# Latent attention in a two-layer block: 128 weight columns a head, keys and values apart, and the rotation read from the product's bank

## The reference

```python
cq = _rmsnorm(b_cq, gq)                       # 384 wide
ckv = _rmsnorm(b_ckv, gkv)                    # 256 wide
qh = _split_heads(cq @ w_uq, MLA_HEADS)       # 8 heads of 64 + 32 columns
q_b = jnp.concatenate([qh[..., :MLA_NOPE], _rope(qh[..., MLA_NOPE:], pos)], axis=-1)
kvh = _split_heads(ckv @ w_ukv, MLA_HEADS)    # 8 heads of 64 key + 64 value columns
k_rope = _rope(b_kr[:, None], pos)            # 32 columns, shared by the heads
k_b = jnp.concatenate([kvh[..., :MLA_NOPE],
                       jnp.broadcast_to(k_rope, (B, MLA_HEADS, S, MLA_ROPE))], axis=-1)
yb = mla_attention(q_b, k_b, kvh[..., MLA_NOPE:])
```

## Time and profile before

| | us |
|---|---|
| time, median of 3 runs | 1920.81 |
| the runs | 1924.45, 1920.81, 1919.28 |
| span of the profiled execution | 1919.6 |
| TensorE busy | 1839.1 |
| VectorE busy | 1327.5 |
| ScalarE busy | 959.1 |
| GpSimd busy | 61.7 |

### The profile page before, as it was taken

How to read it: one execution, slowest core, us unless ns; L and a number is a source line. 1 busy time by engine, 2 the same in 40 slices (tenths; PEclk the granted TensorE clock), 3 DMA queues, 4 the chain that set the end, 5 groups by cost and what they waited for, 6 DMA issues and landing times.

```text
span 1919.6 us, 34151 instructions
## 1 busy us (share of the span) xinstructions
PE 1839.1 (96%) x15048; PEld 1774.3 (92%) x15048; DVE 1327.5 (69%) x1807; ACT 959.1 (50%) x1322; POOL 61.7 (3%) x76
## 2 busy tenths in 40 slices
PE   7999999899989997999999999999999999999998
PEld 7988989799879997999999899999999999899998
DVE  5667777766776777766676867666766676857664
ACT  5565555445645545544456345444544456345443
POOL 0000100000001001000000010001000000010000
PEclk9999999899999998999899999999999899999998
DMA  7445355473463563666456345666566456245662
GB/s 314 176 173 211 149 214 209 166 284 139 179 236 138 188 245 139 237 260 258 165 215 242 114 151 179 256 254 242 192 258 255 170 218 241 112 152 176 250 257 108
DMA packets 59283, 389.69 MB, mean 203 GB/s; under 512 B 6656, under 2 KB 9472, under 8 KB 15232
## 3 DMA queue, kind: packets, MB, share of 16 engines
q1 hardware_dynamic: 59136, 387.52, 53.5%
HBM read 386.45 MB, written 1.05 MB: 202 GB/s over the span
## 4 chain that ended last, share of the span: by engine, by line
PE 65%; DVE 22%; ACT 11%; issue 1%; DMA 1%; SPq 0%; DVEq 0%; ACTq 0%
PE banks L781 16%; PE banks L782 15%; PE banks L783 15%; DVE weights_split L934 9%; ACT weights_split L928 5%; PE bank L782 4%; PE bank L783 4%; PE bank L781 4%; DVE weights L914 1%; ACT map L1369 1%; DVE xbc L2388 1%; ACT map L1375 1%; DVE map_stat L1561 1%; DMA weights<-in_weights 1%; PE banks L984 1%
## 5 line engine op out<-in xcount | busy, mean ns | idle before, releaser
L934 DVE TENSOR_TENSOR weights_split<-weights,weights_split 128x2048 fp32r<-128x2048 f32 (+3 forms) x306 | 656.6, 2147 | 337.9 <-ACT weights_split L928 336.6
L928 ACT CAST weights_split<-weights 128x2048 fp32r<-128x2048 f32 (+3 forms) x306 | 542.4, 1776 | 96.4 <-PE bank L783 70.3
L781 PE MATMUL banks<-u,weights_split 128*128 128x256 f32 (+1 forms) x1648 | 463.0, 281 | 6.9 <-DVE weights_split L934 3.6
L782 PE MATMUL banks<-u,weights_split 128*128 128x256 f32 (+1 forms) x1648 | 458.8, 278 | 0.0
L783 PE MATMUL banks<-u,weights_split 128*128 128x256 f32 (+1 forms) x1648 | 458.5, 278 | 0.0
L781 PE MATMUL banks<-x,weights_split 128*128 128x256 f32 x1056 | 304.6, 288 | 28.4 <-DVE weights_split L934 10.0
L781 PEld LDWEIGHTS banks<-u,weights_split 128*128 128x128 f32 (+1 forms) x1648 | 310.4, 188 | 9.6 <-DVE weights_split L934 4.0
L782 PEld LDWEIGHTS banks<-u,weights_split 128*128 128x128 f32 (+1 forms) x1648 | 310.6, 188 | 0.4
L783 PEld LDWEIGHTS banks<-u,weights_split 128*128 128x128 f32 (+1 forms) x1648 | 310.6, 188 | 0.4
L782 PE MATMUL banks<-x,weights_split 128*128 128x256 f32 x1056 | 298.4, 283 | 0.0
L783 PE MATMUL banks<-x,weights_split 128*128 128x256 f32 x1056 | 298.1, 282 | 0.0
(11 more groups left out here) (339 smaller groups left out, 3023.8 us busy)
## 6 DMA issues: line engine op xcount, KB each, us to landing
weights<-in_weights SPq DMA_DIRECT2D x262, 1024.0 KB, 6.4
weights<-in_ada SPq DMA_DIRECT2D x80, 1024.0 KB, 4.8
weights<-in_weights SPq DMA_DIRECT2D x36, 512.0 KB, 5.0
weights<-in_weights SPq DMA_DIRECT2D x4, 576.0 KB, 6.2
constants_second<-in_constants_second SPq DMA_DIRECT2D x1, 1792.0 KB, 10.0
weights<-in_weights SPq DMA_DIRECT2D x2, 640.0 KB, 7.4
h<-in_x SPq DMA_DIRECT2D x2, 512.0 KB, 5.2
out<-xbc SPq DMA_DIRECT2D x4, 256.0 KB, 2.2
```

Source lines behind the costliest of these rows:

```text
L781: pe.matmul(out, left[0], right[0], start=start, stop=False, **more)
L782: pe.matmul(out, left[0], right[1], start=False, stop=False, **more)
L928: act.do.copy(split[:, 0, 0:n], raw[:, 0:n]).then_inc(*self.act_wrote.inc(("weights", key)))
L934: dve.do.tensor_tensor(split[:, 1, 0:n], raw[:, 0:n], split[:, 0, 0:n].bitcast(F32), ALU.subtract).then_inc(*self.dve_wrote.inc(("weights" ...
```

## The change

The host lays the weights out anew (`rotary_columns`): each head of `uq` gets 128 columns (64 plain, 32 rotary, and the same 32 once more in turned order), the second `b_ckvr` panel gets the turned copy of its 32 rotary columns, and `ukv` has all keys first (512 columns) and then all values. The product itself then holds the turned rows in partitions 96 to 127 of the bank, so `swap16`, `tensor_rope` and the ring slots it took are gone, and VectorE multiplies by the sine straight from the product's bank. VectorE's three operations a pair of heads stay, but they move from a step of their own, one bank late, to the step of the bank, and the first of them now frees the bank instead of ScalarE's copy. For the key's rotary part that first operation moves to the early product (`b_ckvr`), into a tile of its own, `kr_turned`.

`ukv` has two banks of keys instead of four, two heads to each 128 columns: ScalarE copies the even heads from rows 0 to 63 and VectorE the odd ones from rows 64 to 127, and VectorE's copy frees the bank. The values are as before, from contiguous columns. The panels grow: `uq` 1152 to 1536 elements a partition (two a layer), `b_ckvr` 1280 to 1536.

```diff
@@ plan
-        yield ("b_ckvr", l, 1), "w_in", l, 0, start + P, D, 160
+        yield ("b_ckvr", l, 1), "w_ckvr", l, 0, 0, D, 192
...
-        yield from panels("uq", l, "mla_w_uq", Q_LORA, 0, 768, 384)
+        yield from panels("uq", l, "mla_w_uq", Q_LORA, 0, 1024, 512)
@@ mla_q
-            at = 0
             for u in range(2):
                 self.use(("uq", l, u))
                 for b in range(2):
                     self.add("bank", ("uq", l, u), b)
-                    if at:
-                        self.add("rotate_q", l, at - 2)
-                    at += 2
                     yield
                 self.unit_done()
@@ mla_kv
-            self.add("rotate_q", l, HEADS - 2)
             while ("ya", l) not in self.done:
                 yield
             self.add("rotate_k", l)
             self.use(("ukv", l, 0))
-            for b in range(6):
+            for b in range(4):
                 self.add("bank", ("ukv", l, 0), b)
-                if b in (1, 3):
+                if b == 1:
                     yield
@@ tensor_mla_q
-            at = slice((2 * b + j) * 96, (2 * b + j + 1) * 96)
+            at = slice((2 * b + j) * P, (2 * b + j + 1) * P)
             for k in range(kc):
-                last = self.parts(bank[0:96, j * T:(j + 1) * T], (hi[:, k, at], lo[:, k, at]),
+                last = self.parts(bank[:, j * T:(j + 1) * T], (hi[:, k, at], lo[:, k, at]),
@@ tensor_mla_kv
-        if b < 4:
+        if b < 2:
...
-    def tensor_rope(self, raw, heads, name, wrote):
-
-        pe, bank = self.pe, self.turned.take(("rope", name))
-        pe.wait_ge(*wrote)
-        pe.wait_ge(*self.turned.free(("rope", name)))
-        pe.do.matmul(bank[64:96, 0:heads * T], self.k("swap16")[64:96, :], raw, start=True, stop=True).then_inc(
-            *self.filled.inc(("rope", name)))
@@ scalar_first_bank
             act.do.copy(t["b_q"][0:96, h:h + 2, :], self.heads(bank[0:96, :], 2)).then_inc(
                 *self.act_wrote.inc(("b_q", l, h)))
-            self.products.emptied(bank_name, self.act_wrote, ("b_q", l, h))
...
-            if b < 4:
-                act.do.copy(t["b_k"][0:64, 2 * b:2 * b + 2, :], self.heads(bank[0:64, :], 2)).then_inc(
+            if b < 2:
+                act.do.copy(t["b_k"][0:64, 4 * b:4 * b + 3:2, :], self.heads(bank[0:64, :], 2)).then_inc(
                     *self.act_wrote.inc(bank_name))
@@ vector_first_bank
+        elif name == "b_ckvr" and u == 1:
+            dve.wait_ge(self.act_wrote, ("kr", l))
+            self.vector_turned(bank[96:128, T:2 * T], 1, ("k", l), bank_name)
+        elif name == "uq":
+            h = 4 * u + 2 * b
+            dve.wait_ge(self.act_wrote, ("b_q", l, h))
+            self.vector_turned(bank[96:128, :], 2, ("q", l, h), bank_name)
+            self.vector_rotated(t["b_q"][64:96, h:h + 2, :], 2, ("q", l, h), (self.act_wrote, ("b_q", l, h)))
+        elif name == "ukv" and b < 2:
+            dve.wait_ge(self.act_wrote, bank_name)
+            dve.do.tensor_copy(t["b_k"][0:64, 4 * b + 1:4 * b + 4:2, :], self.heads(bank[64:128, :], 2)).then_inc(
+                *self.dve_wrote.inc(("b_k", l, b)))
+            self.products.emptied(bank_name, self.dve_wrote, ("b_k", l, b))
@@ vector_turned, vector_rotated (in place of vector_rope)
+        dve.do.tensor_tensor(self.turned_part(heads, name), self.heads(bank, heads), self.rotary("sin32", heads),
+                             ALU.mult).then_inc(*self.dve_wrote.inc(("rope_sin", name)))
+        self.products.emptied(filled, self.dve_wrote, ("rope_sin", name))
...
+        dve.do.tensor_tensor(raw, raw, self.rotary("cos32", heads), ALU.mult).then_inc(*self.dve_wrote.inc())
+        dve.wait_ge(self.dve_wrote, LAST)
+        dve.do.tensor_tensor(raw, raw, self.turned_part(heads, name), ALU.add).then_inc(
+            *self.dve_wrote.inc(("rope", name)))
@@ rotary_columns (on the host)
+    turned = (np.arange(ROPE) + ROPE // 2) % ROPE
+    uq = np.asarray(a["mla_w_uq"]).reshape(DEPTH, Q_LORA, HEADS, NOPE + ROPE)
+    uq = np.concatenate([uq, uq[..., NOPE + turned]], -1).reshape(DEPTH, Q_LORA, HEADS * P)
+    ukv = np.asarray(a["mla_w_ukv"]).reshape(DEPTH, KV_LORA, HEADS, 2, HD).transpose(0, 1, 3, 2, 4)
```

More of the change, by code:

```diff
@@ L1043, in tensor_first @@
                 self.tensor_values(*at)
-            elif what == "rotate_q":
-                l, h = at
-                self.tensor_rope(self.b["b_q"][64:96, h:h + 2, :], 2, ("q", l, h), (self.act_wrote, ("b_q", l, h)))
-            elif what == "rotate_k":
-                l, = at
-                self.tensor_rope(self.heads(self.b["kr"][64:96, :], 1), 1, ("k", l), (self.act_wrote, ("kr", l)))
             elif what == "mean":
@@ L1085, in tensor_latent_rope @@
         pe.wait_ge(*self.products.free(("bank", key, 0)))
-        for j, (lo_at, hi_at) in enumerate(((0, P), (64, 160))):
+        for j, at in enumerate((slice(0, P), slice(HD, HD + P))):
             for k in range(kc):
-                last = self.parts(bank[0:hi_at - lo_at, j * T:(j + 1) * T],
-                                  (hi[:, k, lo_at:hi_at], lo[:, k, lo_at:hi_at]), (x[:, k, 0, :], x[:, k, 1, :]),
-                                  k == 0, k == kc - 1)
+                last = self.parts(bank[:, j * T:(j + 1) * T], (hi[:, k, at], lo[:, k, at]),
+                                  (x[:, k, 0, :], x[:, k, 1, :]), k == 0, k == kc - 1)
         last.then_inc(*self.filled.inc(("bank", key, 0), ("read", key)))
@@ L1119, in tensor_mla_kv @@
         else:
-            tok = slice((b - 4) * P, (b - 3) * P)
-            v_hi, v_lo = (w.rearrange("p k (h c) -> p k h c", h=HEADS) for w in (hi, lo))
+            tok = slice((b - 2) * P, (b - 1) * P)
             for k in range(kc):
-                last = self.parts(self.heads(bank[:, :], HEADS), (y[:, 7 + k, 0, tok], y[:, 7 + k, 1, tok]),
-                                  (v_hi[:, k, :, NOPE:P], v_lo[:, k, :, NOPE:P]), k == 0, k == kc - 1)
-        last.then_inc(*self.filled.inc(("bank", key, b), *[("read", key)] * (b == 5)))
-    def tensor_rope(self, raw, heads, name, wrote):
-        pe, bank = self.pe, self.turned.take(("rope", name))
-        pe.wait_ge(*wrote)
-        pe.wait_ge(*self.turned.free(("rope", name)))
-        pe.do.matmul(bank[64:96, 0:heads * T], self.k("swap16")[64:96, :], raw, start=True, stop=True).then_inc(
-            *self.filled.inc(("rope", name)))
+                last = self.parts(bank[:, :], (y[:, 7 + k, 0, tok], y[:, 7 + k, 1, tok]),
+                                  (hi[:, k, W:2 * W], lo[:, k, W:2 * W]), k == 0, k == kc - 1)
+        last.then_inc(*self.filled.inc(("bank", key, b), *[("read", key)] * (b == 3)))
     def tensor_scores(self, kind, l, h):
@@ L1153, in tensor_scores @@
                 pe.wait_ge(self.dve_wrote, ("rope", ("q", l, HEADS - 2)))
-                pe.wait_ge(self.act_wrote, ("bank", ("ukv", l, 0), 3))
+                pe.wait_ge(self.act_wrote, ("bank", ("ukv", l, 0), 1))
+                pe.wait_ge(self.dve_wrote, ("b_k", l, 1))
                 pe.wait_ge(self.pool_wrote, ("b_k_rope", l))
@@ L1306, in scalar_first_bank @@
             act.do.copy(t["kr"][64:96, :], bank[64:96, T:2 * T]).then_inc(*self.act_wrote.inc(("kr", l)))
-            self.products.emptied(bank_name, self.act_wrote, ("kr", l))
         elif name == "uq":
@@ L1320, in scalar_first_bank @@
                 act.wait_ge(self.dve_wrote, ("ya", l, 3))
-                act.do.copy(t["b_v"][:, b - 4, :], bank[:, :]).then_inc(*self.act_wrote.inc(bank_name))
-            self.products.emptied(bank_name, self.act_wrote, bank_name)
+                act.do.copy(t["b_v"][:, b - 2, :], bank[:, :]).then_inc(*self.act_wrote.inc(bank_name))
+                self.products.emptied(bank_name, self.act_wrote, bank_name)
         elif name.startswith("gate_"):
@@ L1440, in vector_first @@
                 self.vector_branch_c(*at)
-            elif what == "rotate_q":
-                l, at_h = at
-                self.vector_rope(b["b_q"][64:96, at_h:at_h + 2, :], 2, ("q", l, at_h))
             elif what == "rotate_k":
                 l, = at
-                self.vector_rope(self.heads(b["kr"][64:96, :], 1), 1, ("k", l))
+                self.vector_rotated(self.heads(b["kr"][64:96, :], 1), 1, ("k", l), (self.act_wrote, ("kr", l)))
             elif what == "split_p":
```

39 lines of the change are left out of this document (20 added, 19 removed).

## The result

| | before | after |
|---|---|---|
| time, median (20 runs each) | 1922.15 | 1927.39 |
| ratio, 95% interval | | 1.0028 [1.0020, 1.0036] |
| span of the profiled execution | 1919.6 | 1928.7 |

A forecast was written before the change was run, and what follows sets the result against it. TensorE and VectorE were taken as full side by side in layer 0, TensorE then following VectorE's queue. 3.1 + 1.6 + 0.3 - 0.9 + 0.3 + 1.6 = +6.0 us: span 1925.6, median 1926.8, range 1920.8 to 1931.5.

The forecast's parts named there:

- The walk through VectorE's queue, layer 0: uq to b_z in layer 0: TensorE follows VectorE's queued operations to each freed bank; b_z starts 3.1 us later.
- the late bank: Last uq bank of layer 0: its sine could be held up by slow clock, +0.3 us.
- The copy: VectorE's copy of the odd key heads from a product bank: taken at 0.69 us, 0.41 from below.
- The clock: Where the values start, in both layers: half speed after TensorE's idle stretches, +1.6 us in each layer.
- the clock holds: Rival: waits come as worked out but values start at full clock, +2.5 us, 1923.3; chance 0.27.
- slow work inside a wait: Low clock within TensorE's waits costs nothing, except for the last uq bank of layer 0.
- Layer 1: Layer 1 from the ukv low part: b_z 0.9 us earlier, then +0.3 for transfers and +1.6 for low clock.
- larger panels: Larger uq panels in flight ahead of ukv in layer 1: up to 0.9 us later, taken as 0.3.
- The total: Whole program: +6.0 us, shift staying to the end; median 1926.8, 0.31% above 1920.8.
- The chances of the three outcomes: Whole program: faster by over 0.3% 0.06, within 0.3% 0.48, slower 0.46.
- What was to cost nothing: Early part: layer 1's wait for ScalarE's kr copy fits VectorE's 3.20 us idle; layer 0 0 to 0.3; GpSimd's copies under b_z.
- TensorE sets the pace: Rival: banks freed in time, section takes 13.7 us a layer, 19.9 us gained in all, 1901; chance 0.05.

The follow-up runs named there:

- keys_alone: Kernel before with only the ukv part of the change: two key banks, odd heads copied by VectorE, which frees the bank; 1928.58 us, ratio 1.0030.
- rotation_alone: Changed kernel with the ukv part of before: four key banks, freed by ScalarE; 1922.11 us, ratio 0.9996 to before.
- act_both_kr_early: Changed kernel with ScalarE copying and freeing all query and key banks, and the shared key's rotation ahead of the query products; 1912.78 us, 0.9961 of before.
- kr_early: Changed kernel with only the shared key's rotation and GpSimd's copies moved ahead of the query products; 1928.67 us, ratio 1.0032 to before.
- act_both_kr_first: act_both_kr_early with the cast and low part of the panel two ahead moved behind the keys' copies; 1913.07 us, ratio 0.9954 to before.
- act_keys: Changed kernel, but ScalarE copies the odd key heads too and frees the key banks; 1920.54 us, ratio 1.0000 to before.
- act_both: Changed kernel with ScalarE copying and freeing all query and key banks, VectorE freeing none; 1925.04 us, ratio 1.0016 to before.
- act_turned: Changed kernel with ScalarE copying all 128 query rows and freeing those banks, odd key heads still copied by VectorE; 1930.34 us, 1.0041 of before.

## Why the prediction was right

**The walk through VectorE's queue, layer 0.** Predicted were waits of 2.0, 2.2, 0.7 and 5.0 us; the trace has 1.75, 1.98, 0.47 and 4.96. From the first `uq` low part to `b_z` I worked out 210.94 - 183.46 = 27.5, and 1.9 more for clock and the late bank, 29.4; measured (from VectorE's low part at 182.01) 211.72 - 182.01 = 29.7. The layer's sum was +5.0, and +5.0 it is. That VectorE would have no gap holds: 25.33 of 25.99 us. The absolute places (212.8) come 1.1 us early, because this execution started its `uq` 1.5 us early: it lacks the low clock that before had at 168.4.

**The copy.** Taken at 0.69, bounds 0.41 and 0.69. Each of the four in the trace takes 0.69 (687 to 694 ns), just as taken; in a pair they start 0.61 to 0.65 apart (1.30 us for both, 1.22 to the start of the modulation behind). The Trainium skill ("VectorE: DVE Perf Modes", section "Why PSUM operands drop a tier") holds a float32 source in PSUM to one element a cycle; the trace agrees: the copy takes as long as the two-input sine, and at twice that rate it would have come near the lower bound of 0.41.

**The clock.** +1.6 in each layer; the values took 4.45 us in both (207.27 to 211.72, 581.90 to 586.35) for 2.80 before, +1.65. The rival *the clock holds* is refuted for this execution. The low clock at 576.40 to 579.60 cost nothing, as was said of slow work inside a wait: the key banks came later, and the wait behind them was 2.30 instead of 3.8.

**Layer 1 is the step that was off.** Predicted +1.0 (-0.9 + 0.3 + 1.6), measured -0.8. The queue from the `ukv` low part on was right: predicted 20.5 + 1.6 = 22.1 us to `b_z`, measured 586.35 - 563.83 = 22.5. The term that failed is what lies before it. I took the late transfer of `ukv` as given and added 0.3 for larger panels. Measured from the first `uq` matmul, that low part came 4.47 us later before (559.38 - 554.91) and 2.53 after: -1.9 instead of +0.3, because the cast waited 1.40 us for its transfer and not 3.84. The first of the four waits shows it, 1.35 for 3.4. TensorE had been held up in layer 0 while the transfers were not, which would do this. Two runs fit: keys_alone, as late in layer 0, has no wait for the transfer at all (its cast waits 1.67 us for TensorE), and rotation_alone, hardly late, waits 2.91. One does not: act_both_kr_early is 4.6 us shorter than before in layer 0 and waits only 1.48. So the cause stays open. Without that term the two places would have given 6.4; they gave 4.2.

**The total.** 6.0 predicted; 5.2 by the medians, 5.4 [3.8, 6.9] by the ratio. That it came so near is in part luck: the miss of 1.8 in layer 1 is partly made up by time outside the two places, for which the sum had nothing. The chances of the three outcomes (0.06, 0.48, 0.46) are not those of the rivals either, which add up to 0.05 faster, 0.55 within 0.3% and 0.40 slower; the measured 0.28% lies within. The profiles' 9.1 would have been no better guide than the forecast: 4.9 of it is not in the MLA places. Behind the second first score, the rest of the program took 1329.5 us to the last matmul in after and 1326.1 in before; keys_alone, with the same new wait, has 1326.1 and kr_early 1329.2. So this is not tied to the change. It is the clock: behind the second place before and keys_alone have 65 and 66 us at 1.2 GHz, after and kr_early 73 and 76. What picks the longer or the shorter one is open.

**What was to cost nothing.** In layer 1 VectorE waits for ScalarE's copy of `kr` before the modulation, as the walk said (against the earlier trace rows):

```profile
406.05 0.43 DVE L1596 TENSOR_TENSOR kr_turned<-banks,constants_first 32x256 f32<-32x256 f32 x1 [1.74 <-ACT kr L1286]
406.51 1.32 DVE L909 CUSTOM_DVE_ANT_0 weights<-weights,cond,small_parameters 128x1024 f32<-128x1024 f32 x1
...
409.22 2.29 DVE L929 TENSOR_TENSOR weights_split<-weights,weights_split 128x2048 fp32r<-128x2048 f32 x1 [1.38 <-ACT weights_split L923]
```

The modulation is 8.03 us later than before (398.48), the next low part 6.26 (402.96), so some 1.8 us were absorbed in the idle time that had been named, and TensorE did not notice. GpSimd's copies end in time under `b_z`: the first score in after has no wait.

**The price of the rival *TensorE sets the pace*.** 13.7 us a layer from `uq` to `b_z` was its term. act_both_kr_first, where VectorE frees nothing, has 184.48 to 200.28 in layer 0, 15.8, of which 0.69 and 0.81 are waits: 14.3 for 13.7. The term was nearly right, and so was the reason why the change doesn't get there: its banks are freed by an engine without room.

## What to carry to other kernels

When a change lets another engine free a buffer of a short ring, walk that engine's queue instruction by instruction up to the freeing one. Here an instruction of 0.69 us cost 5 us, because low parts, rotations and a modulation stood ahead of it, and moving it ahead of one instruction of 2.2 us took the slowdown away, though not the whole wait. A gain at one place is worth what the next engine lets through: the same early rotation brought no gain in three kernels and 11 to 12 us in a fourth, and of 15.7 us won in the MLA places half reached the end.

## What the runs showed of the hardware

- GpSimd takes 8.53 us in act_keys for eight copies of 32x256 float32 within SBUF, 1.07 us each, where VectorE does an operation of that shape in 0.42. Over all runs the eight take 6.5 to 9.8 us; what makes the difference was not looked into.
- The fall of the clock did not go by the length of one wait. At the same matmul, ahead of layer 0, it fell behind a wait of 2.19 us in before and held behind this one in after (granted clock 1.00 from 168.00 to 172.00):

```profile
167.93 0.36 PE L776 MATMUL banks<-x,weights_split 128*128 128x256 f32 x1 [2.30 <-DVE a_qk_then_merged L1493]
```

  In after it also held through waits of 1.75 and 1.98 us and fell behind 4.96; in layer 1 it fell behind 3.19, recovered and fell again behind 2.30; in before it held behind 2.42. After the waits of 5.42 and 6.26 us in act_both it stayed low for nearly 7 us, twice as long as in after, and around those of 10.67 and 10.21 us in act_turned for 10.2.
- The permutation matmuls and the waits around them cost about as much as the 9.2 us of waits that came for them: rotation_alone, without them, is at 0.9996 [0.9987, 1.0005] of before.
